# State-space rounds of a hybrid encoder layer: both directions in one bank, with the weighting moved off the x operand

## The chip, the cores and the metric

The kernel runs on one core of one Trainium2 chip. The metric is the device time of one execution in microseconds (us). Three runs of the kernel before took 2295.66, 2295.68 and 2299.93 us, the median is 2295.68 us.

## The reference

One bidirectional encoder layer runs on 16 meta tokens followed by 256 prompt tokens and 512 sample tokens (784 columns): half a SwiGLU network, a mixer with two branches, half a SwiGLU network, norms. The change lies in the first branch of the mixer, the chunked Mamba-2 scan, which is run forwards and backwards. Cut to what matters (Q is the chunk of 128 tokens, 16 heads of width 64 in 4 groups, state 128):

```python
acs = jnp.cumsum((dt * A).reshape(b, c, Q, G, Hg), axis=2)
xdt = (x * dt[..., None]).reshape(b, c, Q, G, Hg, P)
seg = acs[:, :, :, None] - acs[:, :, None, :]
Lm = jnp.exp(jnp.where(mask, seg, -jnp.inf))
CB = jnp.einsum('bctgn,bcsgn->bctsg', Cc, Bc)
y_diag = jnp.einsum('bctsg,bctsgh,bcsghp->bctghp', CB, Lm, xdt)
...
y_bwd = _flip(ssd_chunked(_flip(xp), _flip(dtp[:, :, 1]), A[1], _flip(Bp), _flip(Cp)))
y = (y_fwd + y_bwd)[:, npad:] + d_skip.astype(f32)[:, None] * xs
```

So inside a chunk and for one head, the output at t is a sum over s of x(s) times dt(s), times the decay between s and t, times the product of C(t) and B(s). The forward direction takes s up to t, the backward one s from t on, and each has its own dt and its own A.

## The kernel before, in words

The program writes out one instruction stream per engine; the engines meet in semaphores only. A dense product of 128 output columns is a "job": the weights arrive by DMA in `raw`, ScalarE rounds them to `whi` (L1021), VectorE or GpSimd forms the rest `wlo` (`low`, L1910 on VectorE, L2332 on GpSimd), and TensorE multiplies in three products of 8 steps each into one of two PSUM slots (L525).

The scan works by four head groups of four heads, each with six chunks c (0 to 5). While group g is in its rounds, the jobs of group g+1 are interleaved with it. On TensorE (loop at the end of the SSD part) one pass is: round 0 (`ssd_step(0)`), job 1, round 1, job 2, round 2, job 3, round 3, `ssd_turn` (24 transposes of the next group), `ssd_step(4)`, job 4, `ssd_updates` (20 matmul records), job 5, `ssd_carried`, job 0 of the group after. The last group runs its rounds beside five jobs of the next stage (J_PA), which have no convolution.

A unit is a chunk and a direction, u = 2c + d. `S_STEPS` (written out by hand) gives the rounds their units and outputs: round 0 has units 0 to 2, round 1 units 3 to 5 and output 0, round 2 units 6 to 8 and outputs 1 and 2, round 3 units 9 to 11 and output 3, step 4 outputs 4 and 5. For each unit:

- VectorE's `decays` (L2044) writes `rh`, ScalarE's `decays` (L1338, four scaled copies) writes `rl`: the masked dA of four heads, as two parts.
- TensorE (L811) multiplies both by a strict triangle into bank `aux[u % 3]`: the segment sums, 128 x 512.
- ScalarE's `ssd_step` (L1345) takes the exponential into `e[u % 4]`.
- VectorE's `masked` (L2064) multiplies it by the masked product of C and B, `cbm` (written at L2037).
- GpSimd's `steps` (L2402) writes `xdt`, x times dt, 128 x 256, two buffers per direction.
- For an output chunk TensorE adds a transposed carried part (L821) and, per head and direction, `xdt` times `e` (L824). The carried part and the products for both directions end in one bank, `aux[3]`, and VectorE's `gates` (L2055) reads it.

The order on VectorE in round k of the loop: `decays(k)` (for k = 0 it was done before `ssd_carried`), `low` of job k+1, `gates` of the outputs of round k, `convolve(k)` of the next group (L1981, L1983), `masked(k)`; in round 3 `masked` comes ahead of `convolve`. Then `scan_vectors` (small copies), `gates` of 4 and 5, `low` of job 5, `ssd_updates` (L2006 to L2012), `weighted` (L2072 to L2077), `decays(0)` of the next group, `low` of job 0, `ssd_carried` (L2019 to L2037, its end is `cbm`), `conv_vectors` (three small copies, L1973). The order on ScalarE in round k: `ssd_split(k)`, `decays(k)`, `convolved(k-1)` (SiLU), `ssd_read(k)`, `ssd_step(k)`; after round 3 `ssd_turn` (L1329) reads the transposes into `xbt`. GpSimd has `steps(0)` to `steps(3)`, then `ssd_weighted` (L2394, ten products 16 or 128 x 256 into `xw`). These lines set it:

```python
S_UNITS = [(c, d) for c in range(NC) for d in range(2)]
S_STEPS = [((0, 1, 2), ()), ((3, 4, 5), (0,)), ((6, 7, 8), (1, 2)), ((9, 10, 11), (3,)), ((), (4, 5))]
Y_STEP = [1, 2, 2, 3, 4, 4]
```

Of the kernel before, what the change touches and what calls it, by code (L numbers as in the profile page):

```python
# [13 lines left out]
P = 128  # L14
# [13 lines left out]
TAPS = 5  # L28
# [90 lines left out]
def build(nc, x_prompt, x_sample, meta_tokens, ffn1_norm, ffn1_w_gate_up, ffn1_w_down, mix_norm, w_in,  # L119
# [3 lines left out]
    with ctx:  # L123
# [58 lines left out]
        def ffn_mem(new, t, H):  # L182
# [30 lines left out]
            xdt=[[new(f"xdt{s}{d}", [P, 2 * P]) for d in range(2)] for s in range(2)],  # L213
# [25 lines left out]
        xws = [m_s["xw"][:, n, :] for n in range(4)] + [m_s["co"][n // 3][:, 2 * P * (n % 3):2 * P * (n % 3 + 1)] for n in range(6)]  # L239
        cbm = m_s["prev"][1].rearrange("p c (d t) -> p d c t", d=2)  # L240
# [64 lines left out]
        xdt_ok, y_mm, yz_ok, ya_ok = sem("xdt_ok"), sem("y_mm"), sem("yz_ok"), sem("ya_ok")  # L305
# [195 lines left out]
        def _(pe):  # L501
# [238 lines left out]
            def ssd_turn(G, first=0, last=NC + 2):  # L740

                wait(pe, co_ok, 4, 3, G)
                for n in range(first, last):
                    k, t = (N_META, CO_META[n]) if n < 2 else (P, CO_CHUNK[n - 2])
                    if n >= 3:
                        wait(pe, tr_ok, NC + 2, n - 2, G)
                    else:
                        wait(pe, exp_ok, 2 * NC, n - 2, G)
# [4 lines left out]
            def ssd_updates(G):  # L753

                wait(pe, exp_ok, 2 * NC, 0, G)
# [42 lines left out]
            def ssd_step(k, G):  # L798
# [3 lines left out]
                for u in units:  # L802
                    if u == 2:
                        wait(pe, cbm_ok, 4, 4, G)
                    c, d = S_UNITS[u]
                    wait(pe, rh_ok, 2 * NC, u + 1, G)
                    wait(pe, rl_ok, 2 * NC, u + 1, G)
                    if u >= 3:
                        wait(pe, exp_ok, 2 * NC, u - 2, G)
                    for p, v in enumerate((m_s["rh"], m_s["rl"])):  # L810
                        mm = pe.matmul(aux[u % 3][:, :], strict[d][:, :], v[u % 3][:, :, :], start=(p == 0), stop=(p == 1))  # L811
                    mm.then_inc(seg_mm, 1)
                for c in outs:
                    wait(pe, wy_ok, 2 * NC, 2 * c + 2, G)
                    wait(pe, xdt_ok, 2 * NC, 2 * c + 2, G)
                    wait(pe, yz_ok, 2 * NC, 2 * outs[0], G)
                    wait(pe, yoff_ok, 1, 1, G)
                    for q in range(2):
# [3 lines left out]
                        for hh in (2 * q, 2 * q + 1):  # L822
                            for d in range(2):
                                mm = pe.matmul(aux[3][PD * (hh % 2):PD * (hh % 2 + 1), h:h + P], m_s["xdt"][c % 2][d][:, PD * hh:PD * (hh + 1)],  # L824
                                               m_s["e"][(2 * c + d) % 4][:, hh, :], start=False, stop=(d == 1), skip_group_check=True)
# [187 lines left out]
        def _(act):  # L1013
# [309 lines left out]
            def ssd_turn(G):  # L1323
                for n in range(NC + 2):
                    k = N_META if n < 2 else P
                    if n >= 2:
                        wait(act, xdt_ok, 2 * NC, 2 * (n - 1) - 2 * NC, G)
# [13 lines left out]
            def ssd_step(k, G):  # L1341
                for u in S_STEPS[k][0]:
                    wait(act, seg_mm, 2 * NC, u + 1, G)
                    wait(act, y_mm, 4, Y_STEP[(u - 4) // 2] if u >= 4 else 0, G)
# [1146 lines left out]
```

## Time and profile before

| | |
|---|---|
| median of three runs | 2295.68 us |
| the profiled execution, its own time | 2296.97 us |
| its span in the profile | 2295.4 us |
| TensorE clock granted | 0.995 of full speed |
| TensorE busy | 2243.4 us, 98% of the span |
| VectorE busy | 1457.2 us, 63% |
| ScalarE busy | 1019.1 us, 44% |
| GpSimd busy | 373.2 us, 16% |
| stretch of the scan's rounds | 661.5 to 962 us of the span |

The profiled execution's own time is 1.6 us above its span, and 1.3 us above the median. Start times in rows are microseconds from the span's start. A row of the timeline merges instructions of one line that follow each other; in brackets stands how long the engine was idle before it and what released it. A matmul on f32 data shows as two records. A duration holds what an instruction waited inside the engine, too, so one that was held up by something else than a semaphore shows as a long one.

### The profile page before, as it was taken

How to read it: one execution, taken by the hardware profiler on the slowest of the kernel's cores; microseconds unless marked ns; L12 is line 12 of the kernel's file. 1: busy time of each engine (PE TensorE's matmuls, PEld its weight loads, DVE VectorE, ACT ScalarE, POOL GpSimd, SP SyncE). 2: the span in 40 equal slices, each digit the busy share in tenths (PEclk: the TensorE clock that was granted, in tenths of full speed). 3: DMA queues.
4: the chain of work that ended last, by engine and by line, in shares of the span. 5: the costliest groups of instructions: out<-in, count | busy, mean ns of one | idle time of the engine just before them, and what ended most of it. 6: DMA issues, size and time to landing. Idle time of an engine off the chain costs nothing.

```text
span 2295.4 us, 36398 instructions
## 1 busy us (share of the span) xinstructions
PE 2243.4 (98%) x13156; PEld 2001.7 (87%) x13156; DVE 1457.2 (63%) x2331; ACT 1019.1 (44%) x1659; POOL 373.2 (16%) x257
## 2 busy tenths in 40 slices
PE   8999999998999999999999999999999999999998
PEld 6999999997888787888888888888888899899997
DVE  7677676777879889423555555552246667677676
ACT  6333242334454754623555665644234334242345
POOL 2000000001012201133333333322333000000000
PEclk9999999999999999999999999999999999999999
DMA  3222221213211111132111111111342222231212
GB/s 121 67 74 56 66 81 55 73 37 108 68 34 32 37 46 37 47 92 83 47 47 46 46 46 46 44 31 48 104 133 67 70 75 56 61 86 55 73 38 92
DMA packets 252289, 144.65 MB, mean 63 GB/s; under 512 B 5728, under 2 KB 248592, under 8 KB 252192
## 3 DMA queue, kind: packets, MB, share of 16 engines
q1 hardware_dynamic: 249072, 130.63, 20.5%
q0 software_dynamic: 2352, 12.58, 1.6%
q8 instruction: 62, 1.02, 0.2%
q14 instruction: 35, 0.29, 0.0%
q10 hardware_dynamic: 768, 0.13, 0.0%
HBM read 133.89 MB, written 9.44 MB: 62 GB/s over the span
## 4 chain that ended last, share of the span: by engine, by line
PE 78%; DVE 11%; issue 5%; ACT 3%; POOL 1%; DMA 0%; ACTq 0%; DVEq 0%; POOLq 0%; SPq 0%
PE slot L525 33%; PE aux L556 22%; PE slot L605 14%; DVE ca L1983 1%; DVE wlo L1910 1%; PE aux L932 1%; PE aux L900 1%; POOL wlo L2332 1%; PE aux L824 1%; PE aux L914 1%; PE aux L811 1%; PE aux L925 1%; PE slot L693 1%; PE aux L889 1%; DVE wlo L1678 1%
## 5 line engine op out<-in xcount | busy, mean ns | idle before, releaser
L2332 POOL TENSOR_TENSOR wlo<-raw,whi 128x1024 fp32r<-128x1024 f32 (+1 forms) x100 | 232.2, 2322 | 1027.7 <-ACT whi L1021 1027.7
L525 PE MATMUL slot<-xh,whi 128*128 128x256 f32 (+1 forms) x1360 | 364.9, 350 | 10.3 <-DVE wlo L1910 3.7
L525 PE MATMUL slot<-xh,wlo 128*128 128x256 f32 (+1 forms) x1360 | 351.2, 340 | 0.0
L525 PE MATMUL slot<-xl,whi 128*128 128x256 f32 (+1 forms) x1360 | 350.1, 339 | 0.0
L525 PEld LDWEIGHTS slot<-xh,whi 128*128 128x128 f32 x1360 | 249.3, 188 | 52.6 <-issue 16.5
L525 PEld LDWEIGHTS slot<-xh,wlo 128*128 128x128 f32 x1360 | 255.6, 188 | 30.1
L525 PEld LDWEIGHTS slot<-xl,whi 128*128 128x128 f32 x1360 | 255.4, 188 | 29.8
L556 PE MATMUL aux<-th,whi 128*128 128x392 f32 (+1 forms) x640 | 221.1, 345 | 9.0 <-ACT work L1138 5.0
L1112 ACT ACTIVATE whi<-work 128x512 fp32r<-128x512 f32 x220 | 135.2, 624 | 198.6 <-DVE work L1699 105.0
L556 PE MATMUL aux<-tl,whi 128*128 128x392 f32 (+1 forms) x640 | 216.6, 338 | 0.0
L556 PE MATMUL aux<-th,wlo 128*128 128x392 f32 (+1 forms) x640 | 216.4, 338 | 0.0
L1678 DVE TENSOR_TENSOR wlo<-work,whi 128x512 fp32r<-128x512 f32 x220 | 151.6, 690 | 79.5 <-ACT whi L1112 79.4
L1021 ACT ACTIVATE whi<-raw 128x1024 fp32r<-128x1024 f32 (+1 forms) x129 | 125.6, 974 | 143.2 <-PE slot L525 128.7
L556 PE MATMUL aux<-xh,whi 128*128 128x392 f32 (+1 forms) x480 | 162.5, 339 | 2.4 <-DVE prod L1751 2.4
L556 PE MATMUL aux<-xl,whi 128*128 128x392 f32 (+1 forms) x480 | 162.2, 338 | 0.0
L556 PE MATMUL aux<-xh,wlo 128*128 128x392 f32 (+1 forms) x480 | 162.1, 338 | 0.0
L605 PE MATMUL slot<-ah,whi 128*128 128x272 f32 (+1 forms) x608 | 157.8, 341 | 2.1 <-DVE al L1720 1.4
L605 PE MATMUL slot<-ah,wlo 128*128 128x272 f32 (+1 forms) x608 | 157.0, 340 | 0.0
L605 PE MATMUL slot<-al,whi 128*128 128x272 f32 (+1 forms) x608 | 156.9, 339 | 0.0
L556 PEld LDWEIGHTS aux<-th,whi 128*128 128x128 f32 x640 | 120.1, 188 | 20.4 <-issue 10.7
L1769 DVE SCALAR_TENSOR_TENSOR gate<-slot,rs 128x784 f32<-128x784 f32 (+1 forms) x76 | 73.4, 966 | 101.1 <-PE slot L605 101.0
L605 PEld LDWEIGHTS slot<-ah,whi 128*128 128x128 f32 x608 | 113.3, 188 | 17.6 <-issue 3.2
(346 smaller groups left out, 4344.7 us busy)
## 6 DMA issues: line engine op xcount, KB each, us to landing
raw<-in_w_in SPq DMA_DIRECT2D x81, 512.0 KB, 3.9
raw<-in_ffn_w_gate_up SPq DMA_DIRECT2D x48, 512.0 KB, 4.2
work<-in_ffn_w_gate_up SPq DMA_DIRECT2D x40, 512.0 KB, 4.7
raw<-in_ffn_w_down SPq DMA_DIRECT2D x80, 256.0 KB, 3.1
raw<-in_ssd_w_proj SPq DMA_DIRECT2D x8, 512.0 KB, 4.0
raw<-in_hg_w_proj SPq DMA_DIRECT2D x8, 512.0 KB, 3.9
raw<-in_w_out SPq DMA_DIRECT2D x8, 512.0 KB, 4.0
h_spill<-h POOLq DMA_DIRECT2D x1, 3072.0 KB, 10.8
```

What stands on the lines that cost most here:

```text
L525: mm = pe.matmul(slot[b][:, PC + u:PC + v], w[b][:, t, :], x[:, t, u + off:v + off], start=(t == 0 and p == 0 and q == 0), stop=(t == k - ...
L556: mm = pe.matmul(aux[bank][:, 0:NT - mid], w[:, t, :], x, start=(first and t == 0 and n == 0), stop=(t == HK - 1 and n == 2), skip_group_c ...
L605: mm = pe.matmul(slot[d % 2][:, PC + u:PC + e], quarter(w, v)[:, t, :], x[:, t, u:e], start=(t == 0 and n == 0), stop=(t == PAIRS - 1 and ...
L693: return pe.matmul(slot[j % 2][:, PC + u:PC + v], w[j % 2][:, t, :], x[:, t, u:v], start=first, stop=last)
L811: mm = pe.matmul(aux[u % 3][:, :], strict[d][:, :], v[u % 3][:, :, :], start=(p == 0), stop=(p == 1))
L824: mm = pe.matmul(aux[3][PD * (hh % 2):PD * (hh % 2 + 1), h:h + P], m_s["xdt"][c % 2][d][:, PD * hh:PD * (hh + 1)], m_s["e"][(2 * c + d) % ...
L889: mm = pe.transpose(aux[n % 4][0:k, P * q:P * (q + 1)], v[:, t:t + k], ident[:, :])
L1021: act.activation(whi[s % 2][:, 0:k, :], raw[s % 2][:, 0:k, :], ACT.Copy).then_inc(w_hi, 1)
L1112: act.activation(quarter(whi, v), operand(m_, n % 2), ACT.Copy).then_inc(q_hi, 1)
L1678: dve.tensor_tensor(quarter(wlo, v), operand(m_, n % 2), quarter(whi, v).bitcast(F32), sub).then_inc(q_lo, 1)
L1769: dve.scalar_tensor_tensor(m["t"][:, c0:], slot[b][:, PC + c0:], 0.5, rs[:, c0:], mul, mul).then_inc(dn_free[b], 1)
L2332: pool.tensor_tensor(wlo[s % 2][:, 0:k, :], raw[s % 2][:, 0:k, :], whi[s % 2][:, 0:k, :].bitcast(F32), ALU.subtract).then_inc(w_lo, 1)
```

## The change

- The segment sums of a chunk's two directions go to one bank, `aux[c % 3]`: the forward one starts it, the backward one ends it. The two triangles don't overlap, so the bank holds each direction's sums on its side of the diagonal.
- One exponential per chunk instead of two, into `e[c % 4]`.
- dt moves from x to the mask. ScalarE writes `mk`, the forward half of `cbm` scaled by the forward dt, in four scaled copies 128 x 128 per chunk. GpSimd writes `mb`, the backward half times the backward dt, in one product 128 x 512 per chunk, into the memory of `xw[0..3]`. VectorE adds `mb` to `mk`, waits for its own sum, and multiplies `e` by it.
- TensorE multiplies x itself (`xbt`) by `e`, once per head and chunk.
- The products `xdt` on GpSimd are gone. Waits move accordingly: `ssd_weighted` waits for all of the group's products, GpSimd's and ScalarE's steps wait for `cbm`, ScalarE's reads of the turned chunks wait for the outputs that still read `xbt`.

```diff
@@ tensor: ssd_step
-                    if u == 2:
+                    c, d = S_UNITS[u]
+                    if u == 4:
                         wait(pe, cbm_ok, 4, 4, G)
-                    c, d = S_UNITS[u]
...
-                    if u >= 3:
-                        wait(pe, exp_ok, 2 * NC, u - 2, G)
+                    if d == 0 and c >= 3:
+                        wait(pe, exp_ok, NC, c - 2, G)
                     for p, v in enumerate((m_s["rh"], m_s["rl"])):
-                        mm = pe.matmul(aux[u % 3][:, :], strict[d][:, :], v[u % 3][:, :, :], start=(p == 0), stop=(p == 1))
+                        mm = pe.matmul(aux[c % 3][:, :], strict[d][:, :], v[u % 3][:, :, :], start=(p == 0 and d == 0), stop=(p == 1 and d == 1))
                     mm.then_inc(seg_mm, 1)
                 for c in outs:
-                    wait(pe, wy_ok, 2 * NC, 2 * c + 2, G)
-                    wait(pe, xdt_ok, 2 * NC, 2 * c + 2, G)
+                    wait(pe, wy_ok, NC, c + 1, G)
...
-                            for d in range(2):
-                                mm = pe.matmul(aux[3][PD * (hh % 2):PD * (hh % 2 + 1), h:h + P], m_s["xdt"][c % 2][d][:, PD * hh:PD * (hh + 1)],
-                                               m_s["e"][(2 * c + d) % 4][:, hh, :], start=False, stop=(d == 1), skip_group_check=True)
+                            mm = pe.matmul(aux[3][PD * (hh % 2):PD * (hh % 2 + 1), h:h + P], m_s["xbt"][:, c + 2, PD * hh:PD * (hh + 1)],
+                                           m_s["e"][c % 4][:, hh, :], start=False, stop=True, skip_group_check=True)
@@ scalar: ssd_turn, ssd_step
-                        wait(act, xdt_ok, 2 * NC, 2 * (n - 1) - 2 * NC, G)
+                        wait(act, y_mm, 4, Y_STEP[n - 2] - 4, G)
...
+                wait(act, cbm_ok, 4, 4, G)
                 for u in S_STEPS[k][0]:
-                    wait(act, seg_mm, 2 * NC, u + 1, G)
-                    wait(act, y_mm, 4, Y_STEP[(u - 4) // 2] if u >= 4 else 0, G)
-                    act.activation(m_s["e"][u % 4][:, :, :], aux[u % 3].rearrange("p (h t) -> p h t", h=HPG), ACT.Exp).then_inc(exp_ok, 1)
+                    c, d = S_UNITS[u]
+                    if d == 1:
+                        wait(act, wy_ok, NC, c - 1 if c >= 2 else 0, G)
+                        for h in range(HPG):
+                            ins = act.activation(m_s["mk"][c % 2][:, h, :], cbm[:, 0, c, :], ACT.Copy, scale=m_s["gdt"][:, c, 0, h:h + 1])
+                        ins.then_inc(mk_ok, 1)
+                        wait(act, seg_mm, 2 * NC, u + 1, G)
+                        wait(act, y_mm, 4, Y_STEP[c - 4] if c >= 4 else 0, G)
+                        act.activation(m_s["e"][c % 4][:, :, :], aux[c % 3].rearrange("p (h t) -> p h t", h=HPG), ACT.Exp).then_inc(exp_ok, 1)
@@ vector: masked
-                wait(dve, cbm_ok, 4, 4, G)
                 for u in units:
                     c, d = S_UNITS[u]
-                    wait(dve, exp_ok, 2 * NC, u + 1, G)
-                    v = m_s["e"][u % 4][:, :, :]
-                    dve.tensor_tensor(v, v, cbm[:, d, c, :].unsqueeze(1).broadcast_to([P, HPG, P]), ALU.mult).then_inc(wy_ok, 1)
+                    if d == 0:
+                        continue
+                    m = m_s["mk"][c % 2][:, :, :]
+                    wait(dve, mk_ok, NC, c + 1, G)
+                    wait(dve, mb_ok, NC, c + 1, G)
+                    one(dve.tensor_tensor(m, m, mb[c % 2], ALU.add))
+                    wait(dve, exp_ok, NC, c + 1, G)
+                    v = m_s["e"][c % 4][:, :, :]
+                    dve.tensor_tensor(v, v, m, ALU.mult).then_inc(wy_ok, 1)
@@ gpsimd: ssd_weighted, steps
+                wait(pool, wy_ok, NC, 0, G)
...
+                wait(pool, cbm_ok, 4, 4, G)
+                wait(pool, up_mm, len(S_UPD) // 2, len(S_UPD) // 2, G)
                 for u in S_STEPS[k][0]:
                     c, d = S_UNITS[u]
-                    wait(pool, y_mm, 4, Y_STEP[c - 2] if c >= 2 else 0, G)
-                    pool.tensor_tensor(h4(m_s["xdt"][c % 2][d][:, :]), h4(m_s["xbt"][:, c + 2, 0:2 * P]),
-                                       m_s["gdt"][:, c, d, :].unsqueeze(2).broadcast_to([P, HPG, PD]), ALU.mult).then_inc(xdt_ok, 1)
+                    if d == 1:
+                        wait(pool, wy_ok, NC, c - 1 if c >= 2 else 0, G)
+                        pool.tensor_tensor(mb[c % 2], cbm[:, 1, c, :].unsqueeze(1).broadcast_to([P, HPG, P]),
+                                           m_s["gdt"][:, c, 1, :].unsqueeze(2).broadcast_to([P, HPG, P]), ALU.mult).then_inc(mb_ok, 1)
```

## Rows read from the trace of the kernel before

**Rows 1.** Busy time by stretch: two passes of the loop, then the last group's rounds

```profile
core 0: us, PE busy (x) PEld busy (x) DVE busy (x) ACT busy (x) POOL busy (x), PEclk, DMA share, GB/s
661.50:745.00 83.50, 81.79 (x497) 66.47 (x497) 74.02 (x116) 48.85 (x100) 15.61 (x22) 1.00 0.14 39
745.00:828.50 83.50, 81.78 (x498) 66.52 (x497) 74.01 (x116) 48.84 (x100) 15.61 (x22) 1.00 0.14 38
912.00:962.00 50.00, 50.00 (x327) 40.38 (x326) 21.65 (x36) 35.96 (x66) 6.73 (x9) 1.00 0.21 54
```

**Rows 2.** Timeline of TensorE: where it stood idle in the first pass

```profile
663.62 0.62 PE L525 MATMUL slot<-xh,whi 128*128 128x272 f32 x2 [0.52 <-DVE wlo L1910]
...
697.86 0.50 PE L811 MATMUL aux<-rh,strict 128*128 128x512 f32 x1 [0.23 <-DVE rh L2044]
...
702.12 2.93 PE L750 MATMUL aux<-ident,co 128*16 128x128 f32 x21 [0.34 <-ACT e L1345]
...
735.49 0.60 PE L525 MATMUL slot<-xh,whi 128*128 128x272 f32 x2 [0.62 <-DVE prev L2019]
```

**Rows 3.** Timeline of TensorE: round 1 with output 0, later the first updates

```profile
672.30 0.39 PE L811 MATMUL aux<-rh,strict 128*128 128x512 f32 x1
...
673.69 0.27 PE L821 MATMUL aux<-ident,prev 128*128 128x128 f32 x1
673.89 0.66 PE L824 MATMUL aux<-e,xdt 128*64 128x128 f32 x8
674.49 0.33 PE L821 MATMUL aux<-ident,prev 128*128 128x128 f32 x1
674.75 0.67 PE L824 MATMUL aux<-e,xdt 128*64 128x128 f32 x8
675.34 0.62 PE L525 MATMUL slot<-xh,whi 128*128 128x272 f32 x2
...
716.85 2.19 PE L765 MATMUL aux<-xw,xbt 16*128 16x256 f32 x8
```

**Rows 4.** The line of the output products: all instructions

```profile
L824 PE MATMUL aux<-e,xdt x384: 272/273/324, 673.9 to 961.5; 128*64 128x128 f32 x192
```

**Rows 5.** Timeline of VectorE from the end of cbm to round 2

```profile
659.95 1.95 DVE L2037 TENSOR_TENSOR prev<-aux,incl 128x512 f32<-128x512 f32 x4
...
662.27 1.23 DVE L1910 TENSOR_TENSOR wlo<-raw,whi 128x1024 fp32r<-128x1024 f32 x1
...
670.13 1.89 DVE L2044 TENSOR_TENSOR rh<-incl,gah 128x512 fp32r<-128x512 f32 x3
...
675.56 0.49 DVE L2055 TENSOR_TENSOR work<-aux,work 128x128 f32<-128x128 f32 x2 [2.40 <-PE aux L824]
...
681.10 1.89 DVE L2064 TENSOR_TENSOR e<-e,prev 128x512 f32<-128x512 f32 x3
682.91 1.89 DVE L2044 TENSOR_TENSOR rh<-incl,gah 128x512 fp32r<-128x512 f32 x3
```

**Rows 6.** Timeline of GpSimd in the first pass

```profile
688.95 3.41 POOL L2402 TENSOR_TENSOR xdt<-xbt,gdt 128x256 f32<-128x256 f32 x4 [11.88 <-PE aux L824]
...
710.10 2.32 POOL L2394 TENSOR_TENSOR xw<-xbt,gw_t 16x256 f32<-16x256 f32 x4 [7.01 <-DVE gw_t L1997]
712.38 3.46 POOL L2394 TENSOR_TENSOR co<-xbt,gw_t 128x256 f32<-128x256 f32 x6
```

**Rows 7.** Timeline of VectorE beside GpSimd, and the same place one pass later

```profile
690.60 4.80 DVE L1983 SCALAR_TENSOR_TENSOR ca<-ci,gw,ca 128x802 f32<-128x802 f32 x4
...
704.83 4.33 DVE L1983 SCALAR_TENSOR_TENSOR ca<-ci,gw,ca 128x802 f32<-128x802 f32 x4
...
710.57 8.08 DVE L1910 TENSOR_TENSOR wlo<-raw,whi 128x1024 fp32r<-128x1024 f32 x1
...
794.03 8.08 DVE L1910 TENSOR_TENSOR wlo<-raw,whi 128x1024 fp32r<-128x1024 f32 x1
```

**Rows 8.** Timeline of ScalarE: the scaled copies, and round 3 up to the turned chunks

```profile
691.29 3.62 ACT L1338 ACTIVATE rl<-incl,gal 128x128 fp32r<-128x128 f32 x12
...
698.64 1.28 ACT L1345 ACT_TABLE_LOAD   x1
699.94 0.60 ACT L1345 ACTIVATE e<-aux 128x512 f32<-128x512 f32 x1
...
702.44 3.16 ACT L1329 ACTIVATE xbt<-aux 16x384 f32<-16x384 f32 x8
```

More of the change, by code:

```diff
@@ L212, in build @@
             xbt=new("xbt", [P, NC + 2, 3 * P]), xw=new("xw", [P, 4, 2 * P]),
-            xdt=[[new(f"xdt{s}{d}", [P, 2 * P]) for d in range(2)] for s in range(2)],
+            mk=[new(f"mk{s}", [P, HPG, P]) for s in range(2)],
             prev=[new(f"prev{d}", [P, NC, 2 * P]) for d in range(2)],
@@ L239, in build @@
         xws = [m_s["xw"][:, n, :] for n in range(4)] + [m_s["co"][n // 3][:, 2 * P * (n % 3):2 * P * (n % 3 + 1)] for n in range(6)]
+        mb = [m_s["xw"][:, 2 * s:2 * s + 2, :].rearrange("p a (h t) -> p (a h) t", t=P) for s in range(2)]
         cbm = m_s["prev"][1].rearrange("p c (d t) -> p d c t", d=2)
@@ L303, in build @@
         cb_mm, cbm_ok, wy_ok = sem("cb_mm"), sem("cbm_ok"), sem("wy_ok")
-        xdt_ok, y_mm, yz_ok, ya_ok = sem("xdt_ok"), sem("y_mm"), sem("yz_ok"), sem("ya_ok")
+        mk_ok, mb_ok, y_mm, yz_ok, ya_ok = sem("mk_ok"), sem("mb_ok"), sem("y_mm"), sem("yz_ok"), sem("ya_ok")
         pa_hi, pa_lo = sem("pa_hi"), sem("pa_lo")
@@ L747, in ssd_turn @@
                     else:
-                        wait(pe, exp_ok, 2 * NC, n - 2, G)
+                        wait(pe, exp_ok, NC, n - 2, G)
                     for q in range(3):
@@ L753, in ssd_updates @@
             def ssd_updates(G):
-                wait(pe, exp_ok, 2 * NC, 0, G)
+                wait(pe, exp_ok, NC, 0, G)
                 wait(pe, yz_ok, 2 * NC, 0, G)
@@ L1991, in scan_vectors @@
                 wait(dve, xw_ok, U, 0, G)
-                wait(dve, xdt_ok, 2 * NC, 0, G)
+                wait(dve, mk_ok, NC, 0, G)
+                wait(dve, mb_ok, NC, 0, G)
                 for dst, src in (("gd", drow), ("gdt", dt_t[:, 0:NC]), ("gcd", cd_t), ("gec", ec_t),
@@ L2095, in _ @@
                 G, N = (0, g), (1, g)
-                own.enter(g, 3 + 4 * (TAPS - 1) + 2 + 7 + 6 + 4 + 3)
+                own.enter(g, 3 + 4 * (TAPS - 1) + 2 + 7 + 6 + 4 + 3 + NC)
                 conv_vectors(N)
```

## The prediction

> **What bounds the kernel now.** I read the busy time by stretch first. In a pass of the loop, 83.5 us long, TensorE is busy 81.8 us, VectorE 74.0, ScalarE 48.8, GpSimd 15.6; in the last group's rounds TensorE is busy all of 50.0 us [rows 1]. So TensorE is the bound, and a matmul that goes is time that goes. But VectorE is only 8 us behind it in the loop, so the next view is where TensorE stood idle: four places, 0.52 + 0.23 + 0.34 + 0.62 = 1.7 us a pass, three behind VectorE and one behind ScalarE [rows 2]. They are small, and each shows a chain that ends about when TensorE gets there. The same rows come back 83.46 us later, at 794.03 against 710.57 [rows 7], so a pass is a period and I sum per pass: three passes, then the last group. Below I count from the start of an event to the next; times in the new kernel are worked out in this way.
>
> **a. Matmuls removed.** Eight L824 records, four products, take from 673.89 to 674.49, 0.60 us, and 674.75 to 675.34, 0.59 [rows 3]. There are 384 records for 192 products [rows 4]; half go, 96 products of 0.149 us: -14.3 us, -3.58 in each of the four groups. All of it lies on TensorE's path. The segment matmuls stay, four of 0.23 us per chunk, only their bank differs, at nothing. The durations in the row (273 ns) overlap; the distance of starts is what counts.
>
> **b. The opening wait of a pass.** `cbm` ends at 661.90, VectorE starts the `wlo` of job 1 at 662.27 and TensorE waits 0.52 us for it [rows 2, 5]. With the change GpSimd, which was idle here, starts its two products `mb` of chunks 0 and 1 the moment `cbm` is there. Their price: a GpSimd product of 128 x 256 takes 3.46/6 = 0.58 us [rows 6], twice the width 1.15. Does GpSimd hold VectorE up? Yes: the four L1983 took 4.80 us beside GpSimd's xdt products and 4.33 without, those four xdt 3.41 instead of 4 x 0.58 = 2.3, and one `wlo` that takes 1.23 us took 8.08 while GpSimd ran ten products after each other and more [rows 5 to 7]. So `wlo` starts when the first `mb` ends, 1.0 us late, or when the second ends, 2.1 late. I take +1.0 for all four groups (range 0 to 2.1), since in most rows the two engines take turns.
>
> **c. Round 1.** VectorE's chain `wlo`, convolution, `masked(0)`, `rh` ended at 672.02, and TensorE needed the third `rh` at 672.76 (two thirds into the 1.39 us of segment sums that start at 672.30): 0.75 to spare [rows 3, 5]. New: the 1.0 of b, 1.15 for the second `mb`, 1.15 for the third, which starts at the first product's end and so meets `rh`; one 0.6 less, for chunk 0 has a sum and a product where three products stood, and 0.1 for the wait between them. That is 2.8 - 0.75 = 2.05 late, of which TensorE is 1.0 late by b already. Bounds 0 to 1.1; I take +0.7.
>
> **d. Round 2.** Round 1 holds units 3 to 5, that is both chunk 1 and chunk 2: four VectorE instructions where three stood, +0.63 (1.89/3) and 0.2 for two waits [rows 5]. In front of TensorE's round 2 stands the chain gates, convolution, `masked(1)`, three `rh`, which ended at 684.80 [rows 5], when TensorE needed it at about 684.9, as its idle 0.23 in the round after shows the same chain just missed [rows 2]. That slack of 0.1, and some 0.2 of meetings with xdt that go, are all there is. And `mb` of chunks 3 and 4 now start inside this chain, each released by a product of it: up to 1.15 us each. Both bounds: 0.3 us with no meeting, 2.6 with two full ones. Take +1.6, as one full meeting and a bit, since a meeting costs less than the whole where VectorE was under way first. Both engines' chains start at the same output of TensorE, so a shorter L824 gives no slack here.
>
> **e. Round 3.** One chunk, two instructions instead of three: -0.6, `mb` of chunk 5 +1.15, xdt meetings gone -0.5. The stall of 0.2 and the stretched sums stay or go: -0.2, bounds -0.5 to +0.4.
>
> **f. The turn.** TensorE's transposes need the bank of chunk 5's exponential. ScalarE in round 3 follows the end of job 3 (697.63, from [rows 2]) with 1.0 of reading the slot, then, as now, table load 1.28 and exponentials of 0.6 [rows 8]. New in between: four scaled copies per chunk, 4 x 3.62/12 = 1.2 us, for two chunks [rows 8]. Sum 1.0 + 1.2 + 1.28 + 0.6 + 1.2 + 0.6 = 5.9; behind it five reads of 3.16/8 = 0.4 and the last transposes, 2.4: the turn ends 8.3 after job 3. Now it ends at 705.05, 7.4 after [rows 2]. So it is 0.9 later, though output 3 is 0.6 shorter and the stall of e is gone: +1.7 that a and e counted as gained is not. Bounds 1.0 to 2.2. Elsewhere ScalarE's copies cost nothing: it gains 6 exponentials a pass (3 us), loses 24 copies (7.2), and is at 49 of 83 us [rows 1]; the cover is its waits for jobs.
>
> **g. The end of a pass.** The 0.62 behind `prev` [rows 2] goes if TensorE is later and VectorE is not: the 8.08 shrinks, since the four xdt behind the ten weights [rows 6, 7] are now released only by `cbm`. -0.6, bounds -0.6 to 0.
>
> The new waits elsewhere I cost at nothing. ScalarE now reads the last two turned chunks only after outputs 4 and 5, with the split of job 5's weights queued behind; job 4 (8.6 us) covers both. GpSimd's ten weights wait for the last product, which VectorE finishes before the small copies that release them now; they end at 715.84, and TensorE takes them at 716.85 [rows 3, 6], so 1 us is their cover, and what f delays on VectorE it delays on TensorE too. No DMA is moved.
>
> **Sum.** A pass: -3.58 + 1.0 + 0.7 + 1.6 - 0.2 + 1.7 - 0.6 = +0.6 us, three times +1.9. The last group has no convolutions, so VectorE is idle there and only a and b count: -2.6. Together -0.7 us, against the profiled execution's 2296.97 us, 1.3 above the median; so 2295.0 us for the median. Almost all of the 14.3 us is spent by chains beside TensorE. About 0.2%, 4.6 us, is what a measurement of this kernel can tell from no change.
>
> **Rivals.** *Light meetings*: GpSimd's products fall beside VectorE instructions that aren't held up. For it: VectorE's PSUM reads were not stretched, and the xdt work (12 x 0.58) goes as 6 x 1.15 comes. Against: the instructions around the release points are `rh` and the mask's, all of SBUF operands. Then c is 0, d 0.3: a pass is -3.58 + 1.0 + 0.3 - 0.2 + 1.7 - 0.6 = -1.4, in all -6.8: 2288.9; without b, 2284.9.
>
> *Full lock at each meeting*: every `mb` holds VectorE for its whole length, c 1.05 and d 2.6: a pass +2.0, in all +3.4: 2299.1 us. The 8.08 speaks for it, the 4.80 against it [rows 7]. The Trainium skill has this as a rule (SBUF — State Buffer, Who interferes with whom): a VectorE instruction with two SBUF inputs and a GpSimd one that reads SBUF take a shared port for the whole instruction, and the second fully blocks. By that rule this rival would be the forecast; the trace agrees with the blocking, not with how long.
>
> *Slower, by GpSimd's price*: no row shows its product at 512 columns with both inputs broadcast. If it takes 2 us and not 1.15, b grows by 0.85 in four groups, c by up to 0.85 and d by 1.7 in three: +11.0, so 2306. It decides from about 1.6 us on, where the sum passes +4.6. Against it: the xdt products had one broadcast input and kept 0.58.
>
> *The removal pays less*: if four records take 0.40 us instead of 0.30 since the weight loads bind, a is -9.5: 2299.8.
>
> **Chances.** Forecast 0.33 (same 0.29, faster 0.04), light meetings 0.28 (faster 0.26, same 0.02), full lock 0.20 (same 0.14, slower 0.06), dear GpSimd product 0.14 (slower), smaller removal 0.05 (same). Faster 0.30, same 0.50, slower 0.20. The range runs from light meetings with part of b gone, 2286, to 2303, half way into the dear product; no more than 2 in 10 is outside.
>
> **What would show it.** L824 with 192 records and 0.30 us per four (a); job 1's wait behind `wlo` at 1.5 us instead of 0.52, with GpSimd's product beside it (b); idle time of L811 behind `rh` of 1.5 to 2 us in round 2 (d); L750 idle behind the exponential or the reads by over 2 us (f); no wait behind `prev` (g). A GpSimd product well off 1.15 us, VectorE's `rh` at 0.68 each beside it, or TensorE's idle time in a pass still at 1.7 us would prove the forecast wrong.

## The result, and the profile after

The kernel after takes 2302.38 us, the median of 15 runs (2299.51 to 2312.9); the kernel before, on the same chips, 2295.84 (2295.28 to 2299.93, 15 runs). The ratio is 1.0032, interval 1.002 to 1.0043: slower by 0.3%. It lies inside the stated range, but not in the likeliest case: 0.7 us less was forecast, and 6.5 more came.

Two things are in these 6.5 us (medians of 15 runs each). The profiled execution of after was its fastest, 2299.51 us (span 2297.4, granted clock 0.996), against 2296.97 of the profiled one before (span 2295.4, clock 0.995): 2.5 us more from the stages. And the 15 runs of after go from clock 0.996 (2299.5 to 2300.3 us, four runs) down to 0.987 (2312.9), so its median is 2.9 us above its fastest; before, the median is 0.6 above. The granted clock is TensorE's, as a share of full speed over the whole span.

The busy time by stretch, after (columns: us, then each engine's busy time with its instruction count, the granted clock, DMA). The stretches are those of [rows 1]:

```profile
core 0: us, PE busy (x) PEld busy (x) DVE busy (x) ACT busy (x) POOL busy (x), PEclk, DMA share, GB/s
661.50:745.00 83.50, 78.11 (x440) 62.14 (x439) 74.19 (x112) 52.63 (x118) 15.44 (x16) 1.00 0.14 39
```

TensorE's busy time fell from 81.8 to 78.1, yet a pass grew from 83.46 to 85.17 us (its first segment sum at 662.00, that of the next pass at 747.17; the other two passes take 84.99 and 84.94). Idle time more than took the place of the work. TensorE's timeline of after shows where (start, duration, line and operands; in brackets the idle time before and who ended it):

```profile
664.86 0.61 PE L526 MATMUL slot<-xh,whi 128*128 128x272 f32 x2 [1.32 <-DVE wlo L1916]
...
675.03 0.27 PE L821 MATMUL aux<-ident,prev 128*128 128x128 f32 x1
675.23 0.44 PE L823 MATMUL aux<-e,xbt 128*64 128x128 f32 x4
675.60 0.33 PE L821 MATMUL aux<-ident,prev 128*128 128x128 f32 x1
...
685.86 0.50 PE L812 MATMUL aux<-rh,strict 128*128 128x512 f32 x1 [0.79 <-DVE rh L2051]
...
687.31 0.51 PE L812 MATMUL aux<-rh,strict 128*128 128x512 f32 x1 [0.72 <-DVE rh L2051]
...
702.72 0.49 PE L751 MATMUL aux<-ident,co 128*16 128x128 f32 x3
703.99 0.49 PE L751 MATMUL aux<-ident,co 128*16 128x128 f32 x3 [0.77 <-ACT e L1351]
705.63 2.44 PE L751 MATMUL aux<-ident,co 128*128 128x128 f32 x18 [1.15 <-ACT e L1351]
...
747.17 0.39 PE L812 MATMUL aux<-rh,strict 128*128 128x512 f32 x1
```

Beside [rows 2], three places grew: behind `wlo` at the opening, 0.52 to 1.32; behind `rh` in round 2, now 0.79 + 0.72; and in the turn, 0.77 + 1.15 behind the exponentials. The chain that feeds round 2 and the opening, VectorE's timeline of after:

```profile
662.70 2.02 DVE L1916 TENSOR_TENSOR wlo<-raw,whi 128x1024 fp32r<-128x1024 f32 x1
...
671.66 2.73 DVE L2051 TENSOR_TENSOR rh<-incl,gah 128x512 fp32r<-128x512 f32 x3
...
683.07 0.68 DVE L2073 TENSOR_TENSOR mk<-mk,xw 128x512 f32<-128x512 f32 x1
683.79 1.41 DVE L2076 TENSOR_TENSOR e<-e,mk 128x512 f32<-128x512 f32 x1
685.13 2.73 DVE L2051 TENSOR_TENSOR rh<-incl,gah 128x512 fp32r<-128x512 f32 x3
...
712.87 5.79 DVE L1916 TENSOR_TENSOR wlo<-raw,whi 128x1024 fp32r<-128x1024 f32 x1
...
720.16 0.76 DVE L2013 COPY prev<-aux 128x256 f32<-128x256 f32 x2 [1.50 <-PE aux L766]
```

and GpSimd's products beside it:

```profile
662.60 3.02 POOL L2418 TENSOR_TENSOR xw<-prev,gdt 128x512 f32<-128x512 f32 x2 [24.03 <-DVE prev L2044]
...
683.24 1.42 POOL L2418 TENSOR_TENSOR xw<-prev,gdt 128x512 f32<-128x512 f32 x1 [9.99 <-DVE e L2076]
685.28 1.42 POOL L2418 TENSOR_TENSOR xw<-prev,gdt 128x512 f32<-128x512 f32 x1 [0.63 <-DVE e L2076]
```

Both GpSimd products of round 2 fall into VectorE's chain. The first stretches VectorE's product L2076 from 0.69 to 1.41, the second the three `rh` from 1.89 to 2.73, and both take 1.42 themselves. ScalarE in round 3, after:

```profile
700.74 1.28 ACT L1347 ACTIVATE mk<-prev,gdt 128x128 f32<-128x128 f32 x4
702.04 1.28 ACT L1351 ACT_TABLE_LOAD   x1
703.33 0.60 ACT L1351 ACTIVATE e<-aux 128x512 f32<-128x512 f32 x1
703.83 1.26 ACT L1347 ACTIVATE mk<-prev,gdt 128x128 f32<-128x128 f32 x4
705.00 0.58 ACT L1351 ACTIVATE e<-aux 128x512 f32<-128x512 f32 x1
```

The four scaled copies of a chunk, 1.28 us, stand ahead of each exponential that TensorE's transposes wait for. Over the whole span TensorE waits 6.0 us for `wlo` L1916 in five waits, 5.7 for the exponential in six, and 4.5 for `rh` in six.

### The profile page after: what moved, and what is told of

Same layout as the page of the kernel before. It is cut to its first block, busy times and chain, and to the rows that moved or that the text cites. A ratio compares the mean times of both kernels' runs of the same rounds, so it can differ in the third digit from the quotient of the medians.

```text
span 2297.4 us, 36134 instructions
## 1 busy us (share of the span) xinstructions
PE 2235.9 (97%) x12964; PEld 1991.1 (87%) x12964; DVE 1468.0 (64%) x2331; ACT 1034.4 (45%) x1731; POOL 373.3 (16%) x233
## 4 chain that ended last, share of the span: by engine, by line
PE 79%; DVE 9%; issue 5%; ACT 4%; POOL 1%; DMA 0%; ACTq 0%; DVEq 0%; POOLq 0%; SPq 0%
PE slot L526 34%; PE aux L557 22%; PE slot L606 13%; PE aux L931 1%; PE aux L899 1%; DVE ca L1989 1%; POOL wlo L2344 1%; PE aux L913 1%; PE aux L924 1%; PE slot L694 1%; PE aux L823 1%; PE aux L888 1%; PE aux L812 1%; DVE wlo L1916 1%; DVE wlo L1684 1%
```

## The experiments

My theory after the result: GpSimd's product costs most in round 2, ScalarE's copies cost the turn, and the two hide each other in part. The rivals: the removed matmuls were worth little, or the lowered clock is chance and not these waits. All ratios are against the kernel before, run beside on the same chip, with their 95% interval. Its median beside them was 2296.87 to 2298.9 us, so between kernels the ratios compare better than the microseconds.

**ScalarE's copies earlier.** The copies no longer wait behind the slot reads, nor stand between two exponentials; they run behind the convolution of the round before.

```
-    def ssd_step(k, G):   # wait(act, cbm_ok) and, per backward unit, wait(act, wy_ok) + 4 scaled copies
+    def mask_half(k, G):  # the same waits and copies, with mk_ok
...
                         convolved(k - 1, N)
+                        mask_half(k, G)
                     ssd_read(k, N)
+                    if not k:
+                        mask_half(k, G)
                     ssd_step(k, G)
```

> The changed kernel with one edit: ScalarE's scaled copies of rounds 1 to 3 stand ahead of its read of the job's slot, where it was idle for 1.15 and 1.99 us in round 3. Theory (the turn waits for ScalarE's chain: read 1.0, copies 1.3, table 1.3, exponential 0.5, copies 1.2, exponential 0.5): TensorE's idle time in front of L751, 0.77 + 1.15 us a pass, falls to about 0.5, a pass is 1.5 us shorter (83.7), the fastest runs near 2295. Rival (the turn is paced by the transposes and their reads, the exponential is only the last semaphore): the pass stays at 85.2 and the time at 2299.5 and more. Second question, the spread: the changed kernel ran between 2299.5 and 2312.9 us, with a granted clock of 0.996 down to 0.987; if idle time of TensorE in the rounds brings the clock down, the spread narrows with each wait removed; if it is the kernel's level of work, it stays.

It took 2300.9 us (2296.95 to 2302.67), ratio 1.0008, 0.9999 to 1.0018, against 1.0032 of after. The wait in the turn is gone altogether, as TensorE's timeline of this kernel shows, while the one of round 2 stayed:

```profile
686.16 0.50 PE L812 MATMUL aux<-rh,strict 128*128 128x512 f32 x1 [0.81 <-DVE rh L2063]
...
705.42 3.47 PE L751 MATMUL aux<-ident,co 128*16 128x128 f32 x24
```

So the copies are the cause of f (the turn). The row alone would be weak, for TensorE also comes to the turn later here, at 705.42 and not 702.72; the kernel with both edits, at full clock, shows a wait of 0.43 in place of 0.77 + 1.15. But the pass of this profile is 85.70 us (662.30 to 748.00), not shorter than 85.17. The busy time by stretch, behind the wait of round 2 (clock in the third column from the right), tells why:

```profile
683.50:687.00 3.50, 2.58 (x13) 1.63 (x11) 3.46 (x4) 3.49 (x9) 2.84 (x2) 1.00 0.01 2
687.00:690.50 3.50, 2.89 (x12) 1.38 (x14) 2.29 (x3) 3.47 (x7) 0.00 (x1) 0.73 0.02 6
690.50:694.00 3.50, 3.50 (x17) 1.97 (x18) 0.80 (x4) 3.48 (x13) 0.00 (x0) 0.50 0.53 146
```

TensorE was idle for 0.92 us of 3.50, then for 0.61, and was granted 0.50 of its clock, 1.2 in place of 2.4 GHz, while it was fully busy again. The waits are paid twice. From the start of the pass to the turn it took 43.12 us, in after 40.72: 2.4 us more, for the clock; the other two passes are as long (85.52, 85.45).

**GpSimd's half left out.** GpSimd weighs only two columns per head, and VectorE adds `m` to itself: the backward direction's weighting is left out of the result.

```
-    pool.tensor_tensor(mb[c % 2], ...)
+    pool.tensor_tensor(mb[c % 2][:, :, 0:2], ...)
...
-    one(dve.tensor_tensor(m, m, mb[c % 2], ALU.add))
+    one(dve.tensor_tensor(m, m, m, ALU.add))
```

> The changed kernel without GpSimd's products: each is cut to 2 columns per head, and VectorE adds the scaled half to itself, so the backward direction's weighting is left out of the result. All waits and all other instructions stay. Theory (GpSimd's products hold VectorE up on the way to wlo of job 1 and to the rh of rounds 1 to 3): the idle time behind rh in round 2 falls from 0.79 + 0.72 to under 0.4 us, job 1's wait behind wlo from 1.32 to 0.5, a pass is about 2.7 us shorter (82.5), the fastest run near 2291.5. Rival (round 2 is late because it holds four mask instructions instead of three, whatever GpSimd does): under 1 us a pass, 2297.

2295.43 us (2292.34 to 2298.5), ratio 0.9991, 0.9981 to 1.0. No wait of L812 behind `rh` was left, and the one of the opening fell from 1.32 to 0.53, its value before the change. So b (the opening) is all GpSimd's, and d (round 2) all but 0.7 of it: round 2's segment sums with their waits take 2.07 us (from 683.90, where job 2 ends, to 685.97), against 3.63 in after and 1.38 before. What it gave was partly lost in the turn, which now waits 1.20 + 1.15 us, and in 700 to 720 the clock is 0.91:

```profile
700.00:720.00 20.00, 17.65 (x100) 13.90 (x99) 14.82 (x26) 11.39 (x20) 6.74 (x10) 0.91 0.19 52
```

This profile also gives the clock's price. The next two passes have the same waits in the turn, 1.20 + 1.15 us, and the full clock behind them: they take 82.53 us each, the first 84.12, of which 0.18 is a longer wait at the pass's end. So the lowered clock cost about 1.4 us in one pass, and the same waits brought it in one pass and not in two.

**GpSimd's half behind `wlo`.** The same work, released only when VectorE has finished the `low` of the round, so that it no longer meets the chain in front of it.

```
     wait(pool, up_mm, len(S_UPD) // 2, len(S_UPD) // 2, G)
+    wait(pool, w_lod, 6, 7 + k, G)
```

> The changed kernel with one wait more: GpSimd's product of round k waits until VectorE has written the wlo of that round, so it runs in the time in which VectorE waits for the output chunk, and at the beginning of the convolution, not beside rh. Theory (what costs is where the products meet VectorE, not that they do): job 1's wait behind wlo is 0.5 again, rh takes 0.68 each, a pass is 2 us shorter (83.2), the fastest runs near 2293.5. Rival (any meeting in VectorE's chain costs the same, the chain from gates to rh is as long wherever the product falls): the pass stays within 0.5 us of 85.2.

2297.11 us (2293.29 to 2299.94), ratio 0.9993, 0.9984 to 1.0002. GpSimd's timeline in this kernel:

```profile
687.21 1.04 POOL L2419 TENSOR_TENSOR xw<-prev,gdt 128x512 f32<-128x512 f32 x1 [10.81 <-DVE wlo L1916]
```

A product that meets nobody takes 1.04 us, and the three `rh` take 1.89 again. The work is the same as in after; only its place had cost round 2 its waits. A pass takes 83.87 us, 1.3 less than in after (the next two 83.93 and 84.94), all three with the clock lowered behind the turn. TensorE's turn in this kernel:

```profile
700.32 0.49 PE L751 MATMUL aux<-ident,co 128*16 128x128 f32 x3
702.01 0.50 PE L751 MATMUL aux<-ident,co 128*16 128x128 f32 x3 [1.20 <-ACT e L1351]
703.65 3.61 PE L751 MATMUL aux<-ident,co 128*128 128x128 f32 x18 [1.15 <-ACT e L1351]
```

The waits are longer than after's, since TensorE now comes earlier and ScalarE doesn't. And the 18 records behind them take 3.61 us where after has 2.44.

**Both edits together.**

> The changed kernel with the edits of the two runs before together. If the two chains add up, a pass is 3.4 us shorter than 85.2 (81.8), under the 83.5 of the kernel before, and the fastest runs are near 2289, 6 us under the kernel before. If one chain takes over when the other goes, it is no better than the better of the two. The spread by the clock: under 5 us if idle time in the rounds was its cause.

2286.17 us (2285.41 to 2289.22), ratio 0.9953, 0.9939 to 0.9967. Against after's median, the first edit alone brought 1.5 us, the second 5.3, the two 16.2. By the ratios it is 0.24%, 0.39% and 0.79%, and the first two sum to 0.63 with an uncertainty of about 0.2, so the medians overstate how much more the pair is than its parts. The passes say why it is more at all. At full clock the first edit would give 83.3 us a pass (an estimate: 85.70 less the 2.4 above), the second 82.7 (84.12 less the 1.4 above, for the same waits in the turn), which adds up to 80.8; both together gave 81.10. The waits are removed about one by one; what a single edit doesn't get is mostly the clock, which falls behind the wait that is left. TensorE's timeline in this kernel has the two places thus:

```profile
684.59 0.50 PE L812 MATMUL aux<-rh,strict 128*128 128x512 f32 x1 [0.37 <-DVE rh L2063]
...
701.06 2.93 PE L751 MATMUL aux<-ident,co 128*16 128x128 f32 x21 [0.43 <-ACT e L1356]
```

A pass is 81.10 us, 2.4 less than before the change: close to the 2.71 that the removed matmuls are worth (a). So the rival that the removal is worth little is out.

**Is it the wait that lowers the clock?** I filled the turn's waits in the kernel with `wlo` first: two needless matmuls ahead of each of the two waits, into a bank that was free.

```
+    s4 = J_SSD + 6 * G[0] + 4
+    pe.wait_ge(slot_free[s4 % 2], lin(s4 // 2, 3, G[1]))
+    for _ in range(2):
+        pe.matmul(slot[s4 % 2][:, BANK:BANK + 2 * P], ones[:, :], m_s["co"][0][:, 0:2 * P], start=True, stop=True)
     wait(pe, exp_ok, NC, n - 2, G)
```

> The kernel of e3_half_after_wlo, with four more matmuls of TensorE in the turn, two in each of the two waits for the exponentials (1.20 and 1.15 us there); they write the free slot and nothing reads them. They take about 0.8 us of each wait, so with the clock at full speed the pass stays at its undisturbed length. e3_half_after_wlo ran between 2293.3 and 2299.9, and its trace shows the granted clock below full speed right behind the turn in each of the three passes. Theory (standing idle there is what brings the clock down): with the filler the clock stays up behind the turn and the median comes from 2297.1 to about 2294. Rival (the clock falls by chance or by the sum of work, not by these waits): median and spread stay, or grow.

2294.08 us (2291.0 to 2295.31), ratio 0.9978, 0.9969 to 0.9987; the kernel without them had 2297.11 (0.9993, 0.9984 to 1.0002). The intervals overlap by a hair, the difference of 0.0015 is just clear of its own noise (about 0.0013), and the clocks bear it out: 0.993 to 0.995 in the 11 runs with the filler, 0.990 to 0.995 in the 11 without. In the profiles the passes are 82.73, 82.53 and 82.54 us against 83.87, 83.93 and 84.94. TensorE does more and is done sooner. Its timeline in the turn:

```profile
700.07 1.03 PE L753 MATMUL slot<-co,ones 128*128 128x256 f32 x4
701.43 0.50 PE L756 MATMUL aux<-ident,co 128*16 128x128 f32 x3 [0.34 <-ACT e L1356]
701.76 1.03 PE L753 MATMUL slot<-co,ones 128*128 128x256 f32 x4
703.08 2.44 PE L756 MATMUL aux<-ident,co 128*128 128x128 f32 x18 [0.28 <-ACT e L1356]
```

and the busy time by stretch, in this kernel

```profile
700.00:720.00 20.00, 19.38 (x116) 14.94 (x114) 17.37 (x29) 11.11 (x20) 7.57 (x11) 1.00 0.20 53
```

and in the one without the filler:

```profile
700.00:720.00 20.00, 17.66 (x104) 13.91 (x104) 15.60 (x26) 12.03 (x21) 8.17 (x12) 0.91 0.20 52
```

The 18 records take 2.44 again, at full clock. I then put the same kind of wait into the kernel before, where nothing else of the change is: copies without a use on ScalarE, ahead of round 3's exponentials.

```
     def ssd_step(k, G):
+        if k == 3:
+            for h in range(5):      # 12 in the second kernel
+                wait(act, junk_ok, 5, h, G)
+                act.activation(m_s["junk"][:, :], incl[0][:, :], ACT.Copy).then_inc(junk_ok, 1)
```

> The kernel before, with five scaled-copy-sized instructions (128 x 128, to a scratch tile) added on ScalarE in front of round 3's exponentials, nothing else changed. Theory for the turn: TensorE waits for the exponential by about 2 us more in each of three passes, a pass is 85.3 instead of 83.5, the fastest runs near 2301. Theory for the clock: the kernel before then gets the spread of the changed one, runs up to 10 us above the fastest with a granted clock of 0.99 and below, and the trace shows it lowered behind the turn. Rival: the spread stays at that of the kernel before, 2295 to 2301, shifted by the 6 us.

2297.32 us (2296.53 to 2300.87), ratio 0.9999, 0.999 to 1.0008: inconclusive. The five copies took only 1.69 us and the wait in the turn was 0.89; the clock stayed full, and a pass took 83.86 us, 0.4 more than before: too little for the ratio to tell. So with twelve:

> The run e8_before_late_exp with twelve of the added instructions instead of five. Five took only 1.69 us, TensorE's wait in the turn grew from 0.34 to 0.89 us, and nothing was seen of the clock: 18.9 us busy of 20 around the turn, where the kernels with a lowered clock had 17.4 to 18.5. Twelve take 4.1 us, so the wait is about 3.3 us and TensorE is busy about 16.8 of 20. Theory for the clock (standing idle brings it down, whatever the change): the trace shows it lowered behind the turn in some of the three passes, and runs lie several us above the fastest, with a granted clock of 0.992 and less. By waits alone the fastest is 3 x 2.9 = 9 us above 2295.6, 2304. Rival (the clock comes down through something else that the changed kernel does): no lowered clock in the rounds, all runs within 4 us.

2308.73 us (2307.42 to 2312.32), ratio 1.0055, 1.0041 to 1.0069. TensorE's timeline in the turn and then its busy time by stretch around it:

```profile
704.71 5.28 PE L751 MATMUL aux<-ident,co 128*16 128x128 f32 x24 [3.28 <-ACT e L1350]
```

```profile
701.00:704.50 3.50, 0.43 (x8) 0.19 (x4) 0.49 (x2) 3.34 (x8) 1.18 (x2) 0.83 0.54 150
704.50:708.00 3.50, 3.29 (x16) 2.92 (x17) 3.36 (x5) 2.99 (x7) 0.00 (x0) 0.50 0.00 0
708.00:711.50 3.50, 3.50 (x28) 2.79 (x26) 3.39 (x7) 2.92 (x6) 0.00 (x0) 0.69 0.00 0
```

The three passes take 88.27, 88.47 and 87.16 us, 13.5 more than before, and 8.8 of it is the longer wait (2.94 each); the rest is about what the clock cost, which is lowered behind the turn in each. So a wait of TensorE alone can lower the clock in the kernel before too. With the filler this shows the waits as the cause of the lowered clock where a profile shows one. It doesn't show when a wait has it: after waits 1.92 us in the turn and 1.51 in round 2 at full clock in its profile.

**Transposes first.** Four records now take 0.37 us where eight had taken 0.60. With T the change from a transposition to the narrow products, and r a record, T + 8r against T + 4r gives r = 0.057 and leaves 0.145 us for the change. So I put both transposes of a chunk ahead of all its products, on top of both edits above.

```
     for q in range(2):
         h = 2 * P * (c % 2) + P * q
         pe.transpose(aux[3][:, h:h + P], yoff[:, c, P * q:P * (q + 1)], ident[:, :])
+    for q in range(2):
+        h = 2 * P * (c % 2) + P * q
         for hh in (2 * q, 2 * q + 1):
```

> The kernel of the run e4_both, with TensorE's order changed within an output chunk: both transposed carried parts first, then the eight product records in a row, instead of transpose, four, transpose, four. In the changed kernel four records take 0.37 us where eight took 0.60 before, so 0.057 a record and 0.145 once per group. Theory (the 0.145 is paid at each change from a transpose to the narrow products): a chunk takes 1.0 us instead of 1.20, 24 chunks save about 3 to 5 us, 2282. Rival (it is paid per head pair or per record, not per change): 1.20 stays and the time stays at 2286.

2282.65 us (2282.26 to 2284.96), ratio 0.9937, 0.9922 to 0.9952. In this form the carried part of each chunk's first half is left out of the result: the second transpose opens its bank anew, so that the products of the first half overwrite what stands there instead of being added to it. The Trainium skill says so (PSUM — Partial Sum Buffer, The four PSUM rules): a matmul that starts a group clears the written marks of the bank, not only of its own columns. This case agrees in that the carried part is missing with a start at each transpose, and there with a start at the first alone. The last kernel keeps the carried part, by starting only at the first transpose:

```
-    pe.transpose(aux[3][:, h:h + P], yoff[:, c, P * q:P * (q + 1)], ident[:, :])
+    pe.matmul(aux[3][:, h:h + P], yoff[:, c, P * q:P * (q + 1)], ident[:, :], is_transpose=True, start=(q == 0), stop=(q == 1))
```

> The order of e5_turns_first with one difference: the second transposed part of an output chunk doesn't start the bank anew, it goes on in it. e5_turns_first left the carried part of the first half out of the result, since the second transpose's start made the bank forget it. The same instructions in the same order, so the time should be that of e5_turns_first, 2282.7, 13 us under the kernel before; TensorE takes 0.90 us for an output chunk, as there, against 1.20 in the changed kernel and 1.65 before. Rival (a transpose without a start is slower or has to wait for the one before): 2284 and more.

2284.89 us (2281.72 to 2285.04), ratio 0.9944, 0.993 to 0.9958: 12 us under the kernel before, and the whole computation. TensorE's timeline in this kernel:

```profile
686.20 0.38 PE L820 MATMUL aux<-ident,prev 128*128 128x128 f32 x2
686.51 0.66 PE L824 MATMUL aux<-e,xbt 128*64 128x128 f32 x8
687.10 0.44 PE L820 MATMUL aux<-ident,prev 128*128 128x128 f32 x2
...
700.83 2.93 PE L751 MATMUL aux<-ident,co 128*16 128x128 f32 x21 [1.32 <-ACT e L1357]
```

A chunk takes 0.90 us (686.20 to 687.10), not 1.20, where 1.0 was expected: the eight products take 0.59 in place of twice 0.37, and the two transposes 0.31 in place of 0.20 and 0.26. So the change back, from products to a transpose, costs as much as the change forth. Of the 7 us that 24 chunks would give, against the kernel with both edits, the profiled spans show 4.2 (2284.4 and 2280.2) and the ratios cannot tell it for certain, since their intervals meet. The rest went where the turn waits 1.32 us again, where that kernel waited 0.43, and round 2 0.70 in place of 0.37: TensorE, sooner there, meets the same chains.

**The product of chunk 2 later.** In the kernel with the transposes first (so with the same part left out), VectorE does `masked` of chunk 2 after the next `rh` and not before.

```
-    masked(k, G)                               # in round 1
+    masked(k, G, (1,) if k == 1 else None)
...
     if k == 2:
+        masked(1, G, (2,))                     # ahead of low
```

> The kernel of e5_turns_first, with VectorE's sum and product for chunk 2 moved from the end of round 1 behind the rh of round 2. Theory (round 2 is late by the four mask instructions in front of rh; in e4_both TensorE still idles 0.37 us there and its segment sums take 1.84 instead of 1.39): both go, 0.8 us a pass, 2.4 us less than e5_turns_first. Rival (VectorE's chain is then late for wlo of job 3 or for output 2): the idle time moves to L526 or L823 and nothing is gained. If both theories hold, this is the best kernel, near 2280.

2286.16 us (2285.24 to 2288.71), ratio 0.9949, 0.9936 to 0.9963, so no gain on 0.9937. The wait behind `rh` went, and the turn's grew from 1.32 to 2.59 us:

```profile
701.52 1.08 ACT L1357 ACTIVATE e<-aux 128x512 f32<-128x512 f32 x2
...
702.17 4.15 PE L751 MATMUL aux<-ident,co 128*16 128x128 f32 x21 [2.59 <-ACT e L1357]
```

ScalarE's chain is not later: its last two exponentials start 38.37 us into the pass (701.52 less 663.15), 38.39 in the kernel without this edit (700.36 less 661.97). It is TensorE that comes to the turn 1.3 us sooner and waits 1.3 more for them. Behind the longer wait the clock is lowered in all three passes (0.83 to 0.85 in the ten microseconds around it; the 21 records take 4.15 us in place of 2.93), so a pass is 81.92 us and not 80.49. The wait changed its place, as the rival said, but to another place than the one it named.

## Why the prediction failed

The terms of the first pass, forecast and measured, all from starts in the timelines of before and after:

| step | forecast | measured |
|---|---|---|
| a, matmuls removed | -3.58 | -2.71 |
| b, opening | +1.0 | +0.8 |
| c, round 1 | +0.7 | +0.1 |
| d, round 2 | +1.6 | +2.25 |
| e, round 3 | -0.2 | -0.36 |
| f, turn | +1.7 | +1.6 |
| g, end of pass | -0.6 | 0 |
| sum | +0.6 | +1.7 |

**The step that failed first is a.** It halved the 0.60 us of eight records and so put the change between transposes and products at nothing. Four take 0.37 (675.23 to 675.60 in after): 0.145 of it is for that change and doesn't depend on their number. The rival that the removal pays less had this size, 0.40 for four; I gave it 0.05. Its words, that the weight loads bind, no run showed.

**b and d** were right in mechanism: one GpSimd product ahead of or beside each link. In d both products of the round hit, 0.72 + 0.84 us on VectorE, and with the 0.7 that stands without GpSimd this is 2.26, near the 2.25 measured. b was taken at 1.0, but its own figures (a product of 1.15 from 661.90 on, `wlo` due at 662.27) give 0.8, which is what came.

**c** rests on a misread row. TensorE takes the third `rh` of round 1 not at 672.76 but two records later, as its timeline of before shows:

```profile
673.22 0.39 PE L811 MATMUL aux<-rh,strict 128*128 128x512 f32 x1
```

So the slack was 1.20 us and not 0.75. And the chain came 1.9 us late in its pass, not 2.8 (the third `rh` ends 12.39 us after the first segment sum in after, 10.47 before); TensorE is 0.8 late by b, and the rest is covered, but for 0.1.

**Light meetings, full lock.** A GpSimd product takes 1.04 us alone and 1.42 at the median of after's 24, not 1.15. Where one met VectorE it held it up by 0.72 to 0.84: `wlo` took 2.02 for 1.22, L2076 1.41 for 0.69, the three `rh` 2.73 for 1.89, and the first convolution step

```profile
664.65 1.41 DVE L1987 TENSOR_SCALAR ca<-ci,gw 128x802 f32<-128x802 f32 x1
```

took 1.41 for 0.63. So the meetings were not light. The rows fit a full block in turns: each instruction waits until the one of the other engine that was there first is done. In the opening the first product (662.60) takes its 1.04 and `wlo` (662.70) 0.80 more than alone, which lets it run when the product ends; the second product takes 2.02, 0.98 more than alone, while `wlo` runs; then L1987 is held for 0.78. In round 2 the product of 683.24 starts inside VectorE's L2073 and takes 0.38 more, and L2076 starts inside the product and takes 0.72 more. That is less than the product's length only because part of it was over when VectorE's instruction came. The Trainium skill's rule (SBUF — State Buffer, Who interferes with whom), an exclusive lock, agrees with these rows to 0.1 or 0.2 us. The prediction's reading that the trace bears out the blocking but not how long was wrong in its second half; what was wrong with the rival of that name is its sizes, a product of 1.15 that costs its whole length each time. The dear product, 2 us, is out at a median of 1.42; the 2.02 of the longest is a wait.

**e and f** came as forecast: the turn takes 5.19 us, from its first record at 702.72 to the next work at 707.91, and took 3.60 before. The first edit showed its cause.

**g** failed by its premise. The `wlo` of the last job did shorten, from 8.08 to 5.79, but VectorE then waited 1.50 us for TensorE's updates, at 720.16 in its timeline above, so the wait behind `prev` stayed: 0.65 us in this pass, 0.48 and 0.47 in the next two, 0.62 before.

**The last group** came out at -2.6, as forecast, by two errors that cancel: a paid 2.7 and not 3.6, and b cost nothing and not 1.0, for without convolutions VectorE's `wlo` starts ahead of GpSimd (917.36 and 917.52).

The sum against the profiled executions: three passes of +0.6 and a last group of -2.6 were to be -0.7. The three passes came to +4.7 (255.10 us from 662.00 to 917.10, against 250.39), the last group to -2.6, and 0.45 us were there before the first of them: +2.5. That is 3.2 of the 7.4 us between 2295.0 and 2302.4, and it turned a little faster into slower.

**What no step had** is the other 4.2: I took after's median to lie 1.3 us below its profiled execution, as before's did; it lies 2.9 above. The forecast counted each wait at its length. That it can also halve the clock of what follows was in no term. For after itself it is inferred, since its profile shows full clock in the passes: its slower runs have the lower clocks, its waits have the size of those in the first and third experiment, which had a lowered clock in their profiles, and filling the wait took it away. How much of the 4.2 us it is stays open, and so does why one run of a kernel loses it and another not. Some of it may be no work of the change: on two other chips the kernel before itself had a median 2.0 and 3.3 us above its lowest run (2297.22 over 2295.23, 2298.9 over 2295.65), and no profile shows where that goes. What only after has is its runs of 2309.6 to 2312.9 us, with clocks of 0.989 and 0.987.

The chances were 0.2 for slower and 0.14 of it for a GpSimd price that didn't come. Slower came by others: by a (0.9 us a pass beside its forecast), d (0.65) and g (0.6), less what c gave back (0.6), and by the clock.

## What to carry to other kernels

When the bound engine loses a few instructions at 97% busy, the gain is only what its feeders leave: look at every chain that ends "just in time", and put new work of an engine that blocks another behind, not ahead of, the link that the bound engine waits for. Take small waits out together: one that is left can bring the clock down behind it and take back what the other gave; with both out, 0.3% over turned into 0.5% under. And price a short run of matmuls by what changes at its ends, not by its count: reordering saved 0.30 us a chunk, halving it 0.45.

## What was not expected of the hardware

- Waits of one to three microseconds in a kernel whose TensorE is 97% busy were followed by its lower clock for some microseconds, 0.50 granted in a stretch where it was fully busy; four needless matmuls a pass, put into the waits, brought 3 us back (2297.11 to 2294.08; ratio 0.9993 to 0.9978). In one profile the same waits in three passes had it in one, at a price of about 1.4 us.
- A change from transposes to the 64-column products costs 0.145 us on TensorE, as much as two and a half records, and the change back about as much again (0.30 us a chunk for one of each).
- GpSimd's product of 128 x 512 takes 1.04 us alone, up to 2.02 where it waits for VectorE first, and holds VectorE up by 0.72 to 0.84.
- A `wlo` of VectorE took 5.79 us beside GpSimd's ten weights in a row, 2.02 beside single products. In such a streak the engines don't take turns: the `wlo` ends 0.46 us before the streak does, before the change (718.65 and 719.11, a streak of 14) as after it (718.66 and 719.12, ten), and GpSimd's last product alone is stretched, to 1.58 us from 0.60. So it got in only ahead of the last one. Why there, no run separates.

Not tried: a shorter ScalarE chain in round 3 in the fastest kernel, where the turn still waits 1.32 us a pass.
